# The forget-gate row of each head: a selecting matmul, or a repeating transfer from DRAM

## The reference, cut to what matters

```
b = jnp.cumsum(fb, axis=-1)
D = jnp.where(causal, b[..., :, None] - b[..., None, :] + ib[..., None, :], -jnp.inf)
inter = b + m[..., None]
m_t = jnp.maximum(inter, D.max(-1))
s_mat = jnp.exp(D - m_t[..., None]) * jnp.einsum('bhtd,bhsd->bhts', qb, kb)
```

## Time and profile before

| | before |
|---|---|
| median of 3 runs | 1061.29 us (1060.44 to 1061.91) |
| the profiled execution | span 1061.5 us, which is its own time here |
| PE busy | 996.4 us, 94% of the span |
| DVE, ACT, POOL busy | 656.1, 466.0, 220.1 us |
| mean granted TensorE clock | 0.980 of full speed |
| all DMA | 71.69 MB, 68 GB/s on the mean |

### The profile page before, as it was taken

The page is one execution under the profiler, slowest core; times in us unless marked ns, Lnnn a source line. Parts: engine busy times, 40 slices in busy tenths (PEclk is TensorE's granted clock), DMA queues, the critical chain, the costliest instruction groups (busy, mean ns, idle before and its releaser), DMA issues.

```text
span 1061.5 us, 13971 instructions
## 1 busy us (share of the span) xinstructions
PE 996.4 (94%) x4661; PEld 769.7 (73%) x4661; DVE 656.1 (62%) x1286; ACT 466.0 (44%) x811; POOL 220.1 (21%) x210
## 2 busy tenths in 40 slices
PE   3399999999999999999999999999999999988995
PEld 2368777777677777778677777777878888866884
DVE  3855796756785764976757976653563333344776
ACT  1133566554465543565554655542644232241221
POOL 1110041442132541223540313530100000001320
PEclk9699999999999999999999999999999999999998
DMA  8612111111111101111011111112841121214222
GB/s 298 220 27 58 41 31 40 31 30 32 60 40 40 30 20 61 42 28 50 20 30 59 40 45 26 31 30 70 264 143 40 40 69 49 81 68 139 80 86 111
DMA packets 77496, 71.69 MB, mean 68 GB/s; under 512 B 4700, under 2 KB 66268, under 8 KB 77436
## 3 DMA queue, kind: packets, MB, share of 16 engines
q1 hardware_dynamic: 73116, 58.31, 18.7%
q0 software_dynamic: 2592, 8.52, 2.4%
q10 hardware_dynamic: 1728, 4.20, 1.0%
HBM read 62.49 MB, written 8.39 MB: 67 GB/s over the span
## 4 chain that ended last, share of the span: by engine, by line
PE 78%; DVE 12%; issue 5%; DMA 2%; ACT 2%; SPq 1%; POOL 0%; DVEq 0%; ACTq 0%; POOLq 0%
PE bank L620 37%; PE bank L600 8%; PE bank L602 8%; PE bank L601 8%; PE bank L738 3%; DVE spL L1463 2%; PE bank L705 1%; PE bank L722 1%; PE bank L724 1%; PE bank L719 1%; PE bank L689 1%; PE bank L717 1%; DVE wL L1300 1%; DMA x_rows<-in_x 1%; DMA a_raw<-in_w_ada 1%
## 5 line engine op out<-in xcount | busy, mean ns | idle before, releaser
L620 PE MATMUL bank<-hH,wH 128*128 128x512 f32 x704 | 282.4, 401 | 0.7 <-DVE wL L1300 0.7
L620 PE MATMUL bank<-hL,wH 128*128 128x512 f32 x704 | 279.8, 397 | 0.0
L620 PE MATMUL bank<-hH,wL 128*128 128x512 f32 x704 | 276.5, 393 | 0.0
L1300 DVE SCALAR_TENSOR_TENSOR wL<-w_raw,wH 128x512 fp32r<-128x512 f32 (+1 forms) x122 | 86.8, 713 | 153.3 <-ACT wH L903 152.2
L620 PEld LDWEIGHTS bank<-hH,wH 128*128 128x128 f32 x704 | 132.7, 189 | 52.7 <-issue 25.0
L620 PEld LDWEIGHTS bank<-hH,wL 128*128 128x128 f32 x704 | 133.0, 189 | 27.7 <-issue 0.7
L620 PEld LDWEIGHTS bank<-hL,wH 128*128 128x128 f32 x704 | 133.0, 189 | 26.6 <-issue 1.5
L554 POOL TENSOR_TENSOR tsum<-tsum,soft 128x512 f32<-128x512 f32 (+3 forms) x80 | 86.4, 1101 | 311.9 <-DVE soft L1457 272.7
L557 POOL TENSOR_TENSOR tsL<-tsum,tsH 128x512 fp32r<-128x512 f32 (+3 forms) x80 | 96.1, 1220 | 133.7 <-DVE tsH L1474 133.7
L903 ACT ACTIVATE wH<-w_raw 128x512 fp32r<-128x512 f32 (+1 forms) x122 | 75.6, 621 | 109.0 <-PE bank L602 75.0
L1450 DVE SCALAR_TENSOR_TENSOR soft<-soft,bank 128x512 f32<-128x512 f32 (+3 forms) x96 | 48.3, 544 | 71.7 <-ACT soft L978 71.3
(11 more groups left out here) (250 smaller groups left out, 1664.8 us busy)
## 6 DMA issues: line engine op xcount, KB each, us to landing
w_raw<-in_w_in SPq DMA_DIRECT2D x104, 256.0 KB, 2.8
a_raw<-in_w_ada SPq DMA_DIRECT2D x16, 512.0 KB, 4.9
x_rows<-in_x SPq DMA_DIRECT2D x8, 512.0 KB, 6.5
raw<-in_w_ada POOLq DMA_DIRECT2D x8, 512.0 KB, 5.8
x_in<-in_x SPq DMA_DIRECT2D x8, 512.0 KB, 3.8
out_y<-res SPq DMA_DIRECT2D x8, 512.0 KB, 2.9
raw<-in_w_out SPq DMA_DIRECT2D x10, 256.0 KB, 3.8
ysb_scratch<-y_stage ACTq DMA_DIRECT2D x8, 256.0 KB, 2.0
```

The costliest lines, as they stand in the source:

```text
L620: ins = t.matmul(proj_ps[half][:], w, a, start=(r == 0), stop=(r == JOB_MM // 2 - 1))
L1300: v.scalar_tensor_tensor(out=wL[:, slot, :, 0:width], in0=w_raw[:, slot, :, 0:width], scalar=scale, in1=wH[:, slot, :, 0:width], op0=ALU.m ...
```

## The change

The row is fetched from DRAM instead.

- Once, in the prologue: when `bm` is made, DVE raises `bm_made`, and POOL stores the four rows to a new scratch tensor `bm_dram` (16 KB).
- In every round SP, behind the loads of job 2 (chunks 4 and 5), waits for that store and for the store of the last head (`yml_stored`), and then starts a transfer that reads row i of `bm_dram` once for each partition, 512 KB in all, and writes it into `m_w`.
- `chunk_weights` waits for that transfer (`bm_in`), adds `h_tok[:, 0]` to `m_w` in place with one instruction of 1024 columns instead of two of 512, and goes on as before.
- The two selecting matmuls of a round, `sel_cur` and its copy go, and the counts of fills and drains with them.

```diff
+    bm_dram = nc.dram_tensor("bm_scratch", (NH, S), F32, kind="Internal").ap()
...
-        sel_cur = it("sel_cur", [P, P])
...
-        M_PRO, M_PER = [10, 9, 1], [13, 13, 8]
-        F_V, F_R, F_MK, F_MV, F_CHUNK, F_HN = 0, 1, 2, 3, 4, 12
+        M_PRO, M_PER = [10, 9, 1], [12, 12, 8]
+        F_V, F_MK, F_MV, F_CHUNK, F_HN = 0, 1, 2, 3, 11
...
                         load(slot, w_in_v[:, 4 * q:4 * q + 4, bass.ds(start, P)], split)
+                    if j == 2:
+                        if isinstance(i, int):
+                            row = bm_dram[i:i + 1, :]
+                        else:
+                            row = bm_dram[bass.ds(i, 1), :]
+                        sp.wait_ge(bm_out, 16)
+                        sp.wait_ge(yml_stored, fixed(i * 16 + 16))
+                        sp.dma_start(m_w[:].rearrange("p c t -> p (c t)"), row.broadcast_to((P, S))).then_inc(bm_in, 16)
...
+            pool.wait_ge(bm_made, 1)
+            pool.dma_start(bm_dram[:, :], bm[0:NH, :]).then_inc(bm_out, 16)
...
-                pe.wait_ge(h_cols, i + 1)
-                for n in range(2):
-                    pe.wait_ge(m_drained[n], m_count(n, i, F_R))
-                    t.matmul(misc_ps[n][:], sel_cur[0:32, :], bm[0:32, halves(n)], start=True, stop=True)\
-                        .then_inc(m_filled[n], 1)
...
                 link(v.tensor_tensor(r_e[:], r_i[:], r_b[:], ALU.subtract))
+                dve.sem_inc(bm_made, 1)
...
-                link(v.tensor_copy(sel_cur[:], sel_all[:, bass.ds(i, 1), :].rearrange("p a b -> p (a b)")))
+                link.wait()
...
             def chunk_weights(i):
-                dve.wait_ge(yml_stored, i * 16 + credit)
-                for n in range(2):
-                    dve.wait_ge(m_filled[n], m_count(n, i, F_R) + 1)
-                    u = h_tok[:, 0, 4 * n:4 * n + 4].unsqueeze(2).to_broadcast((P, 4, P))
-                    v.tensor_tensor(m_w[:, 4 * n:4 * n + 4], misc_ps[n][:].rearrange("p (a b) -> p a b", a=4), u,
-                                    ALU.add).then_inc(m_drained[n], 1)
-                    dve.wait_ge(m_drained[n], m_count(n, i, F_R) + 1)
+                dve.wait_ge(bm_in, i * 16 + 16)
+                u = h_tok[:, 0, :].unsqueeze(2).to_broadcast((P, NC, P))
+                link(v.tensor_tensor(m_w[:], m_w[:], u, ALU.add))
                 v.tensor_scalar(m_w[:], m_w[:], 0.0, None, ALU.min).then_inc(w_sum, 1)
```

More of the change, by code:

```diff
@@ L340, in build_kernel @@
         dve_step = sem("dve_step")
+        bm_made, bm_out, bm_in = sem("bm_made"), sem("bm_out"), sem("bm_in")
         y_in, yb_H, yb_L = [sem("y_in0"), sem("y_in1")], sem("yb_H"), sem("yb_L")
```

## The result

The changed kernel is slower: 1068.1 us median of 6 runs (1065.43 to 1070.46), against 1061.6 (1060.44 to 1064.47) of the kernel before in the same comparison. The ratio is 1.0055, with a 95% interval of 1.0036 to 1.0074. A second comparison on another chip, 12 runs, gave 1067.15 against 1063.16, a ratio of 1.0033 (1.0021 to 1.0044). So the loss is some 3.5 to 6 us by the two ratios. The time was forecast at 1066.7. The profiled execution of the changed kernel was the slowest of its six (1070.46), so the 6.5 us between the two spans may be more than the change costs as a rule.

A forecast was written before the change was run, and what follows sets the result against it. The prediction took DVE's queue up to spL of slot 0 as the bound in rounds 1 and 2. Late transfer +1.4 and clock +1.5 in each, less 0.3 and 0.15 in rounds 0 and 3, gave +5.4: 1066.7 us, range 1060 to 1073.

The forecast's parts named there:

- What bounds the place: Ahead of slot 0's exponents in rounds 1 and 2, PE already waits 1.16 us for DVE's spL, so DVE sets the time.
- The addition and the start of the transfer: In chunk_weights one addition of 1.21 us replaces 1.50, saving 0.28 a round; SP starts the transfer 0.55 us behind chunk 5.
- The landing: The transfer into m_w lands 5.0 us after issue (3.2 to 6.8), making DVE 1.7 us late in round 1.
- A late transfer delays PE one to one: Softplus of slot 0 and spL stand behind DVE's wait for bm_in; net +1.4 us in each of rounds 1 and 2.
- PE's idle: Ahead of slot 0's exponents PE, arriving 2.75 us earlier, would stand idle 5.5 us in round 1.
- The clock: Behind PE's idle in rounds 1 and 2 the granted clock drops, costing +1.5 us in each (0 to 2.5).
- The sum: Over the whole kernel, 2 x (1.4 + 1.5) - 0.3 - 0.15 = +5.4 us, giving 1066.7 from the median.
- Rounds 0 and 3: Transfer in time in round 0, 0.15 us late in round 3; changes of -0.3 and -0.15 us, new PE waits 1.4 to 2.
- In time: Rival: the transfer lands in 3.2 us, unseen; 1063.1 us with +3.0 for the clock, 1060.1 if it holds; chance 0.27.
- As slow as `gate`: Rival: the transfer takes 6.8 us, costing 3.2 us in each of rounds 1 and 2; 1072.7 us in all; chance 0.18.
- PE is the bound after all: Rival: chunk_weights waits for PE's rows, so all 9.5 us come out, 1051.8 us, or 1057.5 in part; chance 0.08.

The follow-up runs named there:

- the version that shortens DVE's queue: The changed kernel with chunk_weights moved from ahead of the softplus of slot 0 to slot 3 of the round; 1055.19 us, ratio 0.9922 to the kernel before.
- the plain transfer: The changed kernel with the transfer reading 128 rows of x, each once, instead of one scratch row 128 times; one run took 1063.9 us.
- the early version: The changed kernel with the transfer started behind the load of chunk 3 instead of chunk 5; 1064.78 us, ratio 1.0018 to the kernel before.
- the two matmuls that nobody reads: The changed kernel with two plain float32 matmuls, results unused, where the selecting ones stood, transfer kept; 1065.24 us against 1063.48 of the kernel before, ratio 1.0015.

## Why the prediction was right, and where it wasn't

- *What bounds the place.* DVE's queue sets the time at `spL` of slot 0, so the removed matmuls are worth nothing by themselves. Shown: 15.30 us to `spL` against 15.02, though the scores start 2.66 us sooner behind job 0; and the version that shortens DVE's queue gets the gain.
- *The addition and the start of the transfer.* One of 1.22 us took the place of 1.50, and the transfer started 0.69 us behind the load of chunk 5 where I took 0.55. Right but for 0.1.
- *The landing.* Mis-sized: 5.0 us predicted, 3.8 measured. The failed argument is that repeating a row costs time; the plain transfer landed no sooner, at 3.9. So the 6.8 us of `gate` weren't owed to its shape; its backlog is what is left. DVE so waited 0.46 us and not 1.7, and `spL` moved by +0.28 and not +1.4. The Trainium skill's fit (DMA: Bandwidth & Descriptors, "Anatomy of one DMA — SWDGE (gpsimd) path"), which is stated there for transfers that GpSimd starts, gives an estimate of 3.2 us. The trace shows 3.8 for this one from SP, 0.6 more, so the estimate was nearer than mine. What the 0.6 are owed to wasn't tried.
- *A late transfer delays PE one to one.* Shown, 4.07 us for 4.07 us.
- *PE's idle.* 5.5 us predicted ahead of the exponents, 3.45 measured. Some 1.1 of the difference is the earlier landing. The rest is mostly PE: the removed matmuls bring it to the exponents 2.0 us earlier and not 2.75, because it waits for the low half of the next weights at 281.57, which I had overlooked. It cost nothing, since PE only waited there instead.
- *The clock.* Right as a mechanism, mis-sized the other way. I took one drop, 1.7 us lost, worth 1.5. Two followed each other in both profiles of the changed kernel, 3.4 us lost, worth 2.2 to 2.8 in a round. One drop, where there was only one, was worth 1.4 to 1.6.
- *The sum.* 2.9 us in each of rounds 1 and 2 were predicted and 3.0 and 3.1 measured, because the two errors cancelled: 1.4 + 1.5 stood for 0.3 + 2.7. The nearness of 1066.7 to 1068.1 is owed to that in part.
- *Rounds 0 and 3.* Transfer in time in both, as said for round 0; waits of 1.13 and 0.95 us where I said 1.4 to 2. Round 0 changed by -0.36 against -0.3. Round 3 changed by -1.73 where I had -0.15, by a drop at 660 that was there in one profile and not in the other.
- *The rivals.* "In time" was half right, since the transfer was nearly so, but its price for the clock was 1.5 a round and the early version, where the transfer is in time, shows it: 1.3 to 1.9 us above the kernel before, where this rival said 1.8. "As slow as `gate`" fell. "PE is the bound after all" fell as well, and the two matmuls that nobody reads show it best.

What stays open: when one drop follows the idle time and when two. A wait of 3.45 us was followed by two in one kernel and a wait of 3.47 by one in another. The traces show a pattern: wherever two or three came, the clock had fallen 0.2 us or more before the wait ended (286.71 against 287.13 in round 1 of the changed kernel, while PE stood idle), and wherever one came it fell at the wait's end or up to 1.9 us behind it. That holds for all twelve waits of 2.9 us and more at the exponents, but no run was made to try it.

## What to carry to other kernels

Before an instruction is taken off the busiest engine, look at its next wait in the timeline: if it already waits there for another engine, the freed time becomes idle, and the chain's share by engine doesn't say so. Idle time on PE can cost more than itself, so where work is removed, see whether the queue of the engine that it then waits for can be shortened in the same change. And the worth of moving data another way may lie in the buffers and banks that it frees, and so in the orders that it allows, more than in the instructions that it saves.

## What the runs showed of the hardware

- In the rounds the granted clock fell to 1.2 GHz in stretches that lost 1.7, 3.4 or 5.1 us of full-clock work: with waits of PE of 1.3 us sometimes 1.7 and sometimes nothing, with 2.9 to 3.5 us 1.7 or 3.4, with 3.8 to 4.2 us 3.4, and with 7.5 us 5.1. In the version with the filled idle it also fell twice, 1.7 us lost each time, with no wait over 0.7 us in the 8 us before.
- A drop that falls where PE is ahead of DVE costs nothing: the round with the filled idle lost 1.7 us of clock and took 153.93 us, against 153.94 without.
- A row of 4 KB read 128 times from DRAM lands in 128 partitions as fast as 128 different rows: 3.8 us against 3.9 for 512 KB, the median of four transfers each.
